# A transformer layer with stick-breaking attention: values in two passes with V's high and low part side by side

## The reference

```
h = rmsnorm(x) ; q_sb,k_sb,v_sb, q_r,k_r,v_r,g_r, gate_sb,gate_ret = split(h @ w_in)
# stick-breaking attention, 8 heads of 64, queries in blocks of 128
z     = q k^T / 8                                   (q, k normalised per head)
a     = sigmoid(z) * prod_{s<j<t} (1 - sigmoid(z_j))   for s < t, else 0
y_sb  = a @ v_sb
y_r   = retention(rotary(q_r), rotary(k_r), v_r), 8 heads, values of 128; per-head rmsnorm, * silu(g_r)
x    += (sigmoid(gate_sb) * (y_sb @ w_branch_sb) + sigmoid(gate_ret) * (y_r @ w_branch_ret)) @ w_out
x    += conv-gated feed-forward (2816) ; x += sigmoid(rmsnorm(x) @ w_pg) * (p @ w_pp)
```

## Time and profile before

| | |
|---|---|
| median of 3 runs | 930.93 us (929.85 to 931.32) |
| profiled execution: time, and its span | 929.76 us, 928.0 us |
| TensorE (PE) busy | 900.2 us, 97%, 4102 matmuls |
| VectorE (DVE), ScalarE (ACT) busy | 512.3 us (55%), 396.3 us (43%) |
| granted clock of TensorE | 1.0 over the span |
| one loop body (a pair) | 74.05 us |
| share of the last-ending chain by engine | PE 85%, ACT 6%, DVE 5% |
| matmul of 512 columns | 390 to 400 ns long, one every 0.23 us |

### The profile page before, as it was taken

One profiled execution on the slowest core, in us unless ns is written; L12 is line 12 of the kernel. 1 busy time (PEld: TensorE's weight loads), 2 busy tenths in 40 slices (PEclk: granted clock), 3 DMA queues, 4 the chain that ended last, 5 costly groups with the idle time before them and its releaser, 6 DMA issues.

```text
span 928.0 us, 11519 instructions
## 1 busy us (share of the span) xinstructions
PE 900.2 (97%) x4102; PEld 727.2 (78%) x4102; DVE 512.3 (55%) x653; ACT 396.3 (43%) x517; POOL 4.0 (0%) x11
## 2 busy tenths in 40 slices
PE   6899989989999999999999999999999999999998
PEld 5677767767767788888878788888888888888786
DVE  6887467557567453333456565665656653334354
ACT  6645656556556362322333533333343332322431
POOL 1000000000000000000000000000000000000000
PEclk9999999999999999999999999999999999999999
DMA  7213213112212243232322323222222333332132
GB/s 275 74 35 131 74 35 116 66 57 102 79 57 79 79 149 113 98 106 90 108 97 91 114 90 112 92 90 104 100 90 90 89 104 99 95 96 90 58 131 78
DMA packets 27913, 88.88 MB, mean 96 GB/s; under 512 B 3792, under 2 KB 4832, under 8 KB 27760
## 3 DMA queue, kind: packets, MB, share of 16 engines
q1 hardware_dynamic: 27232, 85.87, 26.8%
q10 hardware_dynamic: 432, 2.63, 0.8%
q0 software_dynamic: 224, 0.06, 0.0%
HBM read 84.34 MB, written 2.10 MB: 93 GB/s over the span
## 4 chain that ended last, share of the span: by engine, by line
PE 85%; ACT 6%; DVE 5%; issue 2%; DMA 1%; ACTq 0%; SPq 0%; DVEq 0%
PE dense L314 26%; PE dense L316 26%; PE dense L315 26%; ACT fs L586 3%; PE z L365 2%; DVE fs L1155 2%; DVE fs L995 1%; PE aty L391 1%; ACT z L586 1%; PE aty L315 1%; PE aty L316 1%; PE aty L314 1%; PE aty L332 1%; DVE lo L995 1%; DVE w_lo L995 1%
## 5 line engine op out<-in xcount | busy, mean ns | idle before, releaser
L314 PE MATMUL dense<-hi,w_hi 128*128 128x512 f32 x1184 | 473.7, 400 | 9.4 <-DVE lo L998 9.0
L316 PE MATMUL dense<-hi,w_lo 128*128 128x512 f32 x1184 | 462.3, 390 | 0.0
L315 PE MATMUL dense<-lo,w_hi 128*128 128x512 f32 x1184 | 462.2, 390 | 0.0
L995 DVE TENSOR_TENSOR w_lo<-w_f,w_hi 128x1024 fp32r<-128x1024 f32 (+2 forms) x160 | 184.3, 1152 | 224.8 <-ACT w_hi L601 224.3
L314 PEld LDWEIGHTS dense<-hi,w_hi 128*128 128x128 f32 x1184 | 222.9, 188 | 62.1 <-issue 15.8
L316 PEld LDWEIGHTS dense<-hi,w_lo 128*128 128x128 f32 x1184 | 222.8, 188 | 47.4
L315 PEld LDWEIGHTS dense<-lo,w_hi 128*128 128x128 f32 x1184 | 223.1, 188 | 45.3 <-issue 2.6
L601 ACT CAST w_hi<-w_f 128x1024 fp32r<-128x1024 f32 (+2 forms) x160 | 158.5, 991 | 181.2 <-PE dense L316 178.8
L586 ACT ACTIVATE fs<-fs 128x512 f32<-128x512 f32 (+2 forms) x79 | 55.3, 707 | 81.0 <-DVE fs L995 41.8
L995 DVE TENSOR_TENSOR fs<-fs 128x512 f32<-128x512 f32 (+3 forms) x115 | 82.9, 727 | 5.6 <-ACT fs L633 2.2
L995 DVE TENSOR_TENSOR lo<-fs,hi 128x512 fp32r<-128x512 f32 (+3 forms) x63 | 47.9, 765 | 40.5 <-ACT hi L930 20.1
(11 more groups left out here) (71 smaller groups left out, 403.2 us busy)
## 6 DMA issues: line engine op xcount, KB each, us to landing
w_f<-in_w_in SPq DMA_DIRECT2D x52, 512.0 KB, 3.3
w_f<-in_w_up SPq DMA_DIRECT2D x44, 512.0 KB, 3.2
w_f<-in_w_down SPq DMA_DIRECT2D x16, 512.0 KB, 3.5
w_f<-in_w_b SPq DMA_DIRECT2D x8, 512.0 KB, 3.1
w_f<-in_w_out SPq DMA_DIRECT2D x8, 512.0 KB, 3.2
w_f<-in_w_pg SPq DMA_DIRECT2D x8, 512.0 KB, 3.1
w_f<-in_w_down SPq DMA_DIRECT2D x8, 384.0 KB, 3.0
fs<-in_xT SPq DMA_DIRECT2D x4, 512.0 KB, 7.1
```

The costliest lines, as they stand in the source:

```text
L314: mm(out, w1, x1, start=start, stop=False, skip_group_check=skip)
L315: mm(out, w1, x0, start=False, stop=False, skip_group_check=skip)
L316: return mm(out, w0, x1, start=False, stop=stop, skip_group_check=skip)
L995: return nc.vector.tensor_tensor(out, a, b, op).then_inc(done, 1)
```

## The change

The stationary operand of a head's values is now 64 columns of V's high part and 64 of its low part. Tile T_SBV of hi holds head 0 in this form, that of lo head 1 (sb_v, v_turned). Two passes, by the high and the low part of the weights, give in ybank rows 0 to 63 the product with high V and in rows 64 to 127 that with low V. ScalarE copies the whole bank to fs (y_out, into A_YE + hd = 16, 17), a DMA from ScalarE's queue moves the half that lies on the wrong partitions into A_YX = 14 (y_move), VectorE adds the halves of both heads (y_add) and the sum is split in one go for both heads (y_high, y_low). The adding and splitting of pair j take place at the end of the next front(), behind y_square and y_square_low. TensorE waits for s_ysraw (the copy) where it waited for s_yslo; branch_a of the first merge waits for the last y_low; sb_factors(j, 3) waits for s_ysadd of the pair before.

```
@@ TensorE, sb_values
                 if hd == 1 and kb == NT - 1:
-                    pe.wait_ge(s_yslo, 2 * j + 1)
+                    pe.wait_ge(s_ysraw, 2 * j + 1)
                 pe.wait_ge(s_atlo, NT * j + NT - kb)
                 cols = slice(kb * P, (kb + 1) * P)
-                ins = split3(aty[:, 2, kb * P:SEQ], hi[:, T_SBV, cols], lo[:, T_SBV, cols], at_row(hi, hd, kb),
-                             at_row(lo, hd, kb), start=(kb == NT - 1), stop=(kb == 0), skip=True)
+                v = (hi if hd == 0 else lo)[:, T_SBV, cols]
+                mm(aty[:, 2, kb * P:SEQ], v, at_row(hi, hd, kb), start=(kb == NT - 1), stop=False,
+                   skip_group_check=True)
+                ins = mm(aty[:, 2, kb * P:SEQ], v, at_row(lo, hd, kb), start=False, stop=(kb == 0),
+                         skip_group_check=True)
@@ TensorE, r_values; before branch_a(GATE0 + 4, 1, 0)
-                    pe.wait_ge(s_yslo, 2 * j + 2)
+                    pe.wait_ge(s_ysraw, 2 * j + 2)
+            pe.wait_ge(s_yslo, PAIRS)
@@ ScalarE
             def high_v(j, n):
                 act.wait_ge(s_vt, 3 * j + n + 1)
+                if n == 0:
+                    for hd in range(2):
+                        ins = nc.scalar.copy(sb_v(hd)[:, :, 0, :], v_turned(hd))
+                    ins.then_inc(s_vhi, 1)
+                    return
...
-            def y_high(j, hd):
-                rows = slice(64 * hd, 64 * hd + 64)
+            def y_out(j, hd):
                 act.wait_ge(s_ysum, 2 * j + hd + 1)
-                nc.scalar.copy(hi[rows, T_YS + j, :], ybank[rows, :]).then_inc(s_yshi, 1)
+                nc.scalar.copy(fs[:, A_YE + hd, :], ybank).then_inc(s_ysraw, 1)
+            def y_move(j, hd):
+                act.wait_ge(s_ysraw, 2 * j + hd + 1)
+                to, src = slice(64 * hd, 64 * hd + 64), slice(64 - 64 * hd, 128 - 64 * hd)
+                act.dma_start(fs[to, A_YX, :], fs[src, A_YE + hd, :]).then_inc(s_ysmove, 16)
+            def y_high(j):
+                act.wait_ge(s_ysadd, 2 * j + 2)
+                nc.scalar.copy(hi[:, T_YS + j, :], fs[:, A_YE, :]).then_inc(s_yshi, 1)
             def sb_factors(j, i):
...
+                if n == 0 and not isinstance(j, int):
+                    act.wait_ge(s_ysadd, 2 * j)
             def front(j, prev):
                 evac(prev, 8)
+                y_move(prev, 1)
...
                 y_square(prev)
+                y_high(prev)
@@ ScalarE, back and first_back
-                y_high(j, 0)
+                y_out(j, 0)
                 high_rot(j, 0)
...
                 high_rot(j, 1)
-                y_high(j, 1)
+                y_move(j, 0)
+                y_out(j, 1)
@@ VectorE (low_v(j, 0) in two halves likewise; both y_low(j, hd) leave back and first_back)
+            def y_add(j):
+                dve.wait_ge(s_ysmove, 32 * (j + 1))
+                for hd in range(2):
+                    rows = slice(64 * hd, 64 * hd + 64)
+                    tt(fs[rows, A_YE, :], fs[rows, A_YE + hd, :], fs[rows, A_YX, :], ALU.add, s_ysadd)
+            def y_low(j):
+                dve.wait_ge(s_yshi, j + 1)
+                tt(lo[:, T_YS + j, :], fs[:, A_YE, :], hi[:, T_YS + j, :], ALU.subtract, s_yslo)
@@ VectorE, front(j, prev)
                 y_square_low(prev)
+                y_add(prev)
+                y_low(prev)
@@ behind the last pair: ScalarE y_move(last, 1) behind evac(last, 8), y_high(last) behind y_square(last);
@@ VectorE y_add(last), y_low(last) behind y_square_low(last)
```

More of the change, by code:

```diff
@@ L68 @@
 A_AT, A_CP = 14, 16
+A_YE, A_YX = 16, 14
 A_SG = (10, 14, 8)
@@ L133, in build @@
         s_ysum, s_yshi, s_yslo = sem("s_ysum"), sem("s_yshi"), sem("s_yslo")
+        s_ysraw, s_ysmove, s_ysadd = sem("s_ysraw"), sem("s_ysmove"), sem("s_ysadd")
         s_zr, s_zd, s_rahi, s_ralo, s_vr, s_yr = (sem("s_zr"), sem("s_zd"), sem("s_rahi"), sem("s_ralo"), sem("s_vr"),
@@ L185, in r_pair, with sb_v, v_turned @@
             return t[:, at:at + 2, 0:width(i)]
+        def sb_v(hd):
+            return (hi if hd == 0 else lo)[:, T_SBV, :].rearrange("p (b t d) -> p b t d", b=NT, t=2)
+        def v_turned(hd):
+            return misc.rearrange("p (b h d) -> p b h d", b=NT, h=2)[:, :, hd, :]
         def yq(t):
@@ L784, in first_back @@
                 sb_high(0, 0)
-                y_high(0, 0)
+                y_out(0, 0)
                 high_rot(0, 0)
@@ L790, in first_back @@
                 high_rot(0, 1)
-                y_high(0, 1)
+                y_move(0, 0)
+                y_out(0, 1)
                 ahead(0, 8)
@@ L840, in _ @@
             evac(last, 8)
+            y_move(last, 1)
             r_high(last, 0)
@@ L852, in _ @@
             y_square(last)
+            y_high(last)
             raw_gate(2)
@@ L1112, in low_v @@
                 t = (T_SBV, T_RV, T_RV + 1)[n]
+                if n == 0:
+                    for hd in range(2):
+                        ins = nc.vector.tensor_tensor(sb_v(hd)[:, :, 1, :], v_turned(hd), sb_v(hd)[:, :, 0, :],
+                                                      ALU.subtract)
+                    ins.then_inc(s_raw_done, 1)
+                    return
                 nc.vector.tensor_tensor(lo[:, t, :], misc, hi[:, t, :], ALU.subtract).then_inc(s_raw_done, 1)
@@ L1238, in first_back @@
                 turned(0, 0)
-                y_low(0, 0)
                 low_rot(0, 0)
@@ L1245, in first_back @@
                 low_rot(0, 1)
-                y_low(0, 1)
                 ahead(0, 8)
@@ L1287, in back @@
                 turned(j, 0)
-                y_low(j, 0)
                 low_rot(j, 0)
@@ L1293, in back @@
                 low_y(prev)
-                y_low(j, 1)
                 ahead(j, 8)
@@ L1317, in _ @@
             y_square_low(last)
+            y_add(last)
+            y_low(last)
             low((GATE0 + 5) // 3, 2)
```

## The result

The changed kernel takes 940.64 us (median of 5 runs, 939.78 to 942.63) against 930.93 (929.85 to 931.32) for the kernel before: a ratio of 1.0109, 95% interval 1.0098 to 1.0120, slower by about 10 us where 5.2 were forecast. Its profiled execution took 940.36 us with a span of 938.6, against 929.76 and 928.0.

What follows compares the result with a forecast made beforehand. TensorE, busy 97% of a 928.0 us span, was taken as the bound. 928.0 - 4.9 (gain) + 9.4 (three stalls) + 0.7 (tail) = 933.2 us of span, or 936.1 on the median; range 932.5 to 941.

Steps and rivals of the forecast that it cites:

- The saving on TensorE: Third pass of sb_values, 32 matmuls fewer: 5.0 us in all, 1.03 us per pair kept, 4.1 us over four pairs.
- The place and the kind of the loss: y_high, waiting for y_add, stands ahead of evac(j, 2) on ScalarE; TensorE's transposes of V wait it out, nothing caught up.
- Rival D: Half of the stall caught up in the same body's scans and turns, 3 x 1.2 us back: 932.5; chance 0.10.
- What was taken as hidden: Wider y_out copies, halves of high_v and low_v, y_move's DMAs: nothing, up to 0.3 us per pair for DMA issue.
- The tail: After the last pair, branch_b waits for low_y because ScalarE's w_hi cast moves 3.14 us: plus 0.7 us.
- the stall: TensorE's wait at the transposes of V for evac(j, 2): 3.14 us in each of three bodies, 9.4 us.
- the lower end of the gain: Lower bound of the 4.9 us gain: 4.3, without the first pair's gain and with half the rest's roundings against it.
- the first pair's 0.8 us: TensorE's wait for y_low(0, 0) at head 1's first block replaced by one for ScalarE's copy: minus 0.8 us.
- the clock's term: Slow matmuls behind the three stalls at the transposes of V: taken as 0 in the sum.
- rival B: Clock falls after each of the three stalls, 3 x 2.1 us more: 942.4, or 939 if only some; chance 0.13.
- the one idle stretch that is followed by slow matmuls: TensorE's 8.28 us idle at the span's start; the next ten matmuls came 0.44 us apart, costing 2.1 us.
- The longest wait of before: TensorE's 1.9 us wait in the first pair, followed by usual matmul spacing; used against a fall of the clock.

Runs made afterwards that it cites:

- two_pass_only: The kernel before with the third pass of sb_values left out and nothing else changed: 926.39 us, ratio 0.9952.
- hold5: The kernel before with five copies between free float tiles behind y_square(prev) on ScalarE, holding evac(j, 2): 946.07 us, ratio 1.0170.
- late_body: The changed kernel with y_high and y_low behind the next pair's high_v and low_v in the loop only, additions and tail left: 927.23 us, ratio 0.9962.
- late_add_first: The changed kernel with y_add ahead of y_square_low, y_high and y_low behind the next pair's high_v and low_v: 926.42 us, ratio 0.9952.
- add_first: The changed kernel with both additions ahead of y_square_low in the loop only, y_high left in place: 929.00 us, ratio 0.9979.
- hold3: The kernel before with three copies between free float tiles behind y_square(prev) on ScalarE: 938.75 us, ratio 1.0081.

## Why the prediction was off

Right, by its own steps:
- The saving on TensorE. The remaining passes keep their spacing (head 1's last ones start 0.11, 0.12, 0.17 and 0.23 us ahead of the next matmul, as in the earlier trace rows), and 1.03 us per body is kept; two_pass_only shows the absorbed part by itself.
- The place and the kind of the loss: ScalarE's program order in front of evac(j, 2), nothing caught up later in the body. hold5 makes the same stall in the kernel before, late_body and late_add_first remove it. Rival D is out: each body keeps its delay to the last transpose, to within 0.05 us.
- What was taken as hidden is hidden: late_add_first has all of it and no loss.
- The tail, +0.85 for 0.7, low_y ending just too late for branch_b. Forecast by shifting ScalarE's cast at 328.48.

Off by size only: the stall, 3.33 us a body for 3.14. The two additions take 1.40 us and are 0.70 apart, not 0.61 as the row had it for unlike instructions, and y_high wakes 0.13 us after them, not 0.03. Three bodies: 0.6 us.

One bound was added up wrongly, without consequence for the time or the range: the lower end of the gain, 4.3 us, does not follow from its own words. Without the first pair's 0.8 the gain is 4.1, before any rounding.

Wrong: the step that put the clock's term at nothing in the sum, with a chance of 0.13 for rival B. The measured term is 4.0 us, two falls in three bodies. Two sentences carried that step, and both failed.
- "It is less than half of the one idle stretch that is followed by slow matmuls": I read the 8.28 us stretch as if it said something about shorter ones. It does not; it is also the kernel's start, with no matmul before it. Between 1.9 and 8.3 us the trace of before had no row, and the stall lay there.
- "The longest wait of before [...] is followed by the usual spacing": true of that one execution. In the profiled executions of late_add_first, add_first, hold3 and hold5 the same 1.9 us wait is followed by slow matmuls, at a cost of 1.5 us.

The falls cost 4.0 us in the profiled execution of the changed kernel, three quarters of the 5.4 us that were missing; the start (0.7, not the change's), the stall's size and the tail make up the rest. The sum with the falls at the rival's own price would have been 942.4, with the price measured (two falls, 4.0 us) 940.1; 940.64 was measured. The rule of the Trainium skill that I set against the change ("TensorE: Matmul & The Clock Gate", Why this matters for your kernels: no idle gaps of about this size between bursts of matmuls) was the better guide than my single row. The trace agrees with it in bodies 1 and 3 and not in body 2, where the clock stayed up behind 3.47 us; and the runs here show falls behind shorter gaps as well, 2.2 and 1.9 us.

## What to carry to other kernels

A wait between two engines without slack is a place where every instruction put ahead of the releasing one counts in full, however small it is and however idle that engine is on average: put such work behind the release, where the engine waits anyway. Here that is the difference between 940.6 and 926.4 us (ratios 1.0109 and 0.9952) for the same arithmetic. And a stall on TensorE is to be priced twice, by its length and by the slow matmuls that may follow; one profile in which a wait of that size went well is no evidence that it always does.

## What the runs showed of the hardware that I had not expected

- Behind an idle stretch of 1.9 to 3.5 us the granted clock may go to its lower level (matmuls of 512 columns 0.43 us apart in place of 0.23, 1.2 against 2.4 GHz) or stay up, in the same kernel, from one body to the next and from one execution to the next. A fall costs 1.5 us in nine cases out of ten in the table. The tenth, body 1 of the changed kernel, costs 2.5: its transposes are already slow, and 5.7 us pass from their start to the first matmul at the usual spacing, against 3.6 us of slow matmuls in body 3. What decides whether the clock falls within this span of lengths stays open.
- The scatter of the kernel before goes with it: of thirteen executions on one chip, the three with a granted clock of 1.0 took 930.18, 930.29 and 930.66 us, and the ten with 0.997 or 0.998 took 930.77 to 931.55. The means are 0.7 us apart, half of what a fall costs in the traces; none of the ten was profiled, so where their clock fell is not shown.
- Spare matmuls in a stall that can't be removed paid here: about 4 us for 42 of them. For the seven in the first pair a gain is not shown.
- The granted clock over the whole span hardly shows this: 0.995 goes with 4.0 us of falls in the changed kernel. The windows view, asked for short stretches behind each long wait, does.
